# One add fewer on VectorE, two accumulating matmuls more on TensorE, in three deferred layer norms of a decoder step

## What is computed

```python
def _layernorm(x, g, b):
    xf = x.astype(F32)
    mu = jnp.mean(xf, axis=-1, keepdims=True)
    var = jnp.mean(jnp.square(xf - mu), axis=-1, keepdims=True)
    return ((xf - mu) * lax.rsqrt(var + EPS) * g + b).astype(x.dtype)

for layer in range(DEPTH):
    m, ... = _mixer_ab(x, ...) if layer % 2 == 0 else _mixer_cd(x, ...)
    x = _layernorm(DN_ALPHA * x + m, ln_g[layer, 0], ln_b[layer, 0])
    x = _layernorm(DN_ALPHA * x + _ffn(x, ...), ln_g[layer, 1], ln_b[layer, 1])
```

## Time and profile before

| | before |
|---|---|
| median of 3 runs | 1396.12 us (1396.09 to 1396.78) |
| profiled execution | 1397.7 us, its span 1395.9 us |
| mean granted TensorE clock | 0.989 |
| TensorE busy | 1342.1 us (96%) |
| VectorE busy | 815.0 us (58%) |
| ScalarE busy | 452.0 us (32%) |
| GpSimd busy | 594.2 us (43%) |

### The profile page before, as it was taken

One profiled execution on the slowest core, in us unless ns is written; L12 is line 12 of the kernel. 1 busy time (PEld: TensorE's weight loads), 2 busy tenths in 40 slices (PEclk: granted clock), 3 DMA queues, 4 the chain that ended last, 5 costly groups with the idle time before them and its releaser, 6 DMA issues.

```text
span 1395.9 us, 28685 instructions
## 1 busy us (share of the span) xinstructions
PE 1342.1 (96%) x11696; PEld 1268.9 (91%) x11696; DVE 815.0 (58%) x1007; ACT 452.0 (32%) x600; POOL 594.2 (43%) x256
## 2 busy tenths in 40 slices
PE   7999999999999999999899989989999999999994
PEld 7999999999999999999799964469999999999994
DVE  3256775797655553223758999837787555540045
ACT  3332233433333332213423234434443333331132
POOL 2342333355555554343323344004365555554351
PEclk9999999999999999999999999999999999999998
DMA  6222231323333232222788989942222222232301
GB/s 245 61 87 67 77 92 50 94 65 107 79 107 92 90 118 86 101 71 76 275 284 265 329 277 342 360 196 82 86 76 90 90 90 90 90 125 83 99 26 62
DMA packets 84429, 180.81 MB, mean 130 GB/s; under 512 B 25977, under 2 KB 25978, under 8 KB 83842
## 3 DMA queue, kind: packets, MB, share of 16 engines
q1 hardware_dynamic: 83666, 175.82, 38.5%
q0 software_dynamic: 688, 3.92, 0.9%
HBM read 173.66 MB, written 6.05 MB: 129 GB/s over the span
## 4 chain that ended last, share of the span: by engine, by line
PE 86%; DVE 10%; ACT 2%; issue 1%; DMA 1%; SPq 0%; ACTq 0%; DVEq 0%
PE ps L1064 75%; DVE pj L2284 3%; PE ps L1443 2%; PE ps L1211 1%; PE ps L1560 1%; DVE sq L1777 1%; DVE sq L1775 1%; PE ps L1414 1%; PE ps L1545 1%; DMA raw<-in_w_ab_in 1%; ACT sq L541 0%; PE ps L1534 0%; DVE tiny L2358 0%; PE ps L1315 0%; ACT wh L436 0%
## 5 line engine op out<-in xcount | busy, mean ns | idle before, releaser
L900 POOL TENSOR_TENSOR wl<-raw,wh 128x1024 fp32r<-128x1024 f32 (+1 forms) x179 | 492.3, 2750 | 623.7 <-ACT wh L436 623.7
L1064 PE MATMUL ps<-xh,wh 128*128 128x260 f32 x2112 | 436.1, 288 | 16.0 <-DVE xl L1826 9.7
L1064 PE MATMUL ps<-xl,wh 128*128 128x260 f32 x2112 | 430.0, 285 | 0.0
L1064 PE MATMUL ps<-xh,wl 128*128 128x260 f32 x2112 | 429.5, 285 | 0.0
L436 ACT ACTIVATE wh<-raw 128x1024 fp32r<-128x1024 f32 (+1 forms) x179 | 200.0, 1117 | 558.3 <-PE ps L1064 557.5
L1064 PEld LDWEIGHTS ps<-xh,wh 128*128 128x128 f32 x2112 | 331.2, 191 | 22.6 <-issue 16.4
L1064 PEld LDWEIGHTS ps<-xl,wh 128*128 128x128 f32 x2112 | 331.0, 190 | 0.0
L1064 PEld LDWEIGHTS ps<-xh,wl 128*128 128x128 f32 x2112 | 329.7, 190 | 0.0
L1064 PE MATMUL ps<-hh,wh 128*128 128x260 f32 x704 | 142.1, 283 | 0.0
L1064 PE MATMUL ps<-hh,wl 128*128 128x260 f32 x704 | 141.6, 282 | 0.0
L1064 PE MATMUL ps<-hl,wh 128*128 128x260 f32 x704 | 141.3, 282 | 0.0
(11 more groups left out here) (348 smaller groups left out, 1508.7 us busy)
## 6 DMA issues: line engine op xcount, KB each, us to landing
raw<-in_w_f_in SPq DMA_DIRECT2D x88, 512.0 KB, 3.6
pages<-in_cache_kt SPq DMA_DIRECT2D x128, 256.0 KB, 4.2
pages<-in_cache_v SPq DMA_DIRECT2D x128, 256.0 KB, 4.2
raw<-in_w_f_out SPq DMA_DIRECT2D x32, 704.0 KB, 4.0
raw<-in_w_ab_in SPq DMA_DIRECT2D x23, 512.0 KB, 3.6
raw<-in_w_cd_in SPq DMA_DIRECT2D x20, 512.0 KB, 5.1
raw<-in_w_ab_out SPq DMA_DIRECT2D x8, 512.0 KB, 3.5
raw<-in_w_cd_out SPq DMA_DIRECT2D x8, 512.0 KB, 6.2
```

What stands on the lines that cost most here:

```text
L900: nc.gpsimd.tensor_tensor(wl[:, j % SPLIT, 0:b * P], raw[:, j, 0:b * P], wh[:, j % SPLIT, 0:b * P].bitcast(F32), ALU.subtract).then_inc(w_ ...
L1064: mm = nc.tensor.matmul(out[h], w[:, slot, block_at * P:block_at * P + P], rows[k][:, HT * h:end if h else HT], start=start and a, stop=st ...
```

## The change

VectorE stops one add earlier: it signals ln_sq_added once two rows are left (the add of L1776). TensorE multiplies ones with both rows, one after the other in the same accumulator, so `square_sums` has four matmuls in place of two. This happens in the norms before f0_in, cd_in and f1_in. Nothing else is different, and no other instruction changes place.

```diff
                 pe.wait_ge(ln_sq_added, LN_OF[idx] + 1)
                 for h in range(2):
-                    mm = nc.tensor.matmul(ps[:, 4 + h, 0:HT], ones, sq[:, 0, HT * h:HT * h + HT], start=True, stop=True)
+                    for k in range(2):
+                        mm = nc.tensor.matmul(ps[:, 4 + h, 0:HT], ones, sq[:, k, HT * h:HT * h + HT], start=k == 0, stop=k == 1)
                 mm.then_inc(ln_var, 1)
...
                 link(V.tensor_tensor(sq[:, 0:4, :], sq[:, 0:4, :], sq[:, 4:8, :], ALU.add))
-                link(V.tensor_tensor(sq[:, 0:2, :], sq[:, 0:2, :], sq[:, 2:4, :], ALU.add))
-                V.tensor_tensor(sq[:, 0, :], sq[:, 0, :], sq[:, 1, :], ALU.add).then_inc(ln_sq_added, 1)
+                V.tensor_tensor(sq[:, 0:2, :], sq[:, 0:2, :], sq[:, 2:4, :], ALU.add).then_inc(ln_sq_added, 1)
```

## The result

The changed kernel takes 1392.59 us (median of 22 runs, 1390.02 to 1397.92), the kernel before 1396.91 us (22 runs, 1395.09 to 1401.77): ratio 0.9968 with a 95% interval of 0.9959 to 0.9977, so 3.2 to 5.7 us faster, 4.5 in the middle. Runs of one kernel differ by several microseconds, more than the three runs at hand for the prediction had shown. The profiled execution took 1392.94 us, its span is 4.8 us shorter than that of before.

A forecast was written before the change was run, and what follows sets the result against it. TensorE, busy 1342.1 us, bounds the kernel, so only its waits or added work count. Gains of 0.69 + 1.33 + 0.69 = 2.7 us take the median from 1396.12 to 1393.4 us, range 1391.6 to 1395.2.

The forecast's parts named there:

- The place: At the sums of squares in f0_in, cd_in and f1_in: 2.44 us before, 1.745 after, TensorE 0.69 us further on each.
- The waits at tile 6 stay: In f0_in and f1_in VectorE's chain moves 0.69 us with TensorE, so the 1.28 us waits at tile 6 remain.
- cd_in (1.33 us): L1443 starts 1.33 us earlier: 0.69 from the sums, 0.64 from VectorE's chain, with L2173 held by GpSimd's next L900.
- The clock: At L1443 in cd_in: falls to 1.2 GHz behind a 2.75 us wait as before, 1.46 us still lost.
- Clock kept: Rival, chance 0.15: cd_in's shorter wait leaves TensorE at 2.4 GHz, 4.2 us gained, 1391.9.
- The scatter: Spread of the runs shown for the whole kernel, 0.7 us, used in the forecast's own range 1392.7 to 1394.1.
- how the chances were divided at 0.2%: Whole kernel: 2.8 us is distinguishable from no change; faster 0.46, same 0.47, slower 0.07.
- Second add held: Rival, chance 0.03: L1776 starts after GpSimd's L900 and is held, 1.4 us lost per norm, 4.3 in all, 1400.4.
- Not what it says: Rival, chance 0.04: L1178's wait is for a bank or ScalarE and stays, 2.6 us added, 1398.7.
- Eaten by the second wait: Rival, chance 0.16: VectorE's chain meets another hold, TensorE waits longer at L1443 and tile 6; 1394.0 to 1395.4.

The follow-up runs named there:

- the run in which GpSimd waits: Kernel before, three adds and two matmuls kept, but GpSimd's subtraction for the second round's first slot waits for ln_sq_added: 1393.54 us against 1397.88, ratio 0.9973.
- the kernel with four rows: Changed kernel with only VectorE's first add kept and eight matmuls summing four rows: 1397.44 us against 1397.88 for the kernel before, ratio 0.9998.

## Why the prediction was right, and where it was off

**The number.** 1392.59 us is close to the 1393.4 forecast, but luck has a part in that: the kernel before took 1396.91 us beside it and not 1396.12, and the gain is 4.5 us (3.2 to 5.7) where 2.7 was forecast. What was right is the mechanism, place by place.

**The place (0.69 us each): right.** 0.71 us in f0_in and 0.68 in f1_in, each up to tile 6, and 0.69 in cd_in, up to TensorE's arrival at the key slots. The removed add was held by GpSimd, shown by the run in which GpSimd waits (0.70 us). The matmuls cost 0.435 us each, shown by 1.745 us for four and, in the kernel with four rows, 0.44 for each one more.

**The waits at tile 6 stay: right.** 1.26 us each against 1.28 in f0_in and 1.27 in f1_in; 2.5 us for both in the waits, as before.

**cd_in (1.33 us): right, 1.39.** The small adds came when the hold ended and L2173 was caught by the next L900, as forecast. I had the adds held; it was the copy ahead of them, L2191, with one input. The time is the same.

**The clock: the step that was off.** I let the clock fall behind 2.75 us because that is nearer to 3.39 than to 1.3. It fell in 5 of 8 such standstills, and in the profiled execution it didn't. "Clock kept", which I had at 0.15, is neither the rule nor an exception, and an average over runs contains it in part. 2.82 + 0.55 = 3.4 us, inside the interval of 3.2 to 5.7, near its low end. What the middle, 4.5, holds beyond that isn't explained by any run; executions differ by up to 4 us in the attention stretch alone and by 3 us before the first norm (start to the add in f0_in 270.7 to 274.1 us in these traces), and the four sets of runs of the kernel before have medians 1.4 us apart, so it may well be chance. That is argued, not shown.

**The scatter** was taken from three runs (0.7 us). Over 22 runs it is some 7 us. The forecast itself doesn't hang on it, but how the chances were divided at 0.2% does: with gains of clock and scatter on either side, that line was drawn too finely.

**The rivals.** Second add held: no. It starts 1.20 us ahead of L900, as before. Not what it says: the wait is gone with the add. Eaten by the second wait: not in the changed kernel, but the GpSimd run and the one with four rows show the mechanism in cd_in, the first with a copy held and the second with GpSimd 0.05 us ahead.

## What to carry to other kernels

When an instruction on VectorE takes several times what its size wants, look for a GpSimd operation that began before it and ended just ahead of its end, by about the work that its size wants (0.55 us for 520 columns). Taking the instruction out, or letting GpSimd wait for it, is worth the hold and not the work. In f0_in and f1_in letting GpSimd wait gave 1.6 us a place and taking the add out 0.7, since the latter pays with 0.87 us of TensorE's time. In cd_in it was the other way round, 0.7 against 1.4, because the later subtraction held something else. So a hold moved can be a hold kept: trace what the freed engine meets next. And before forecasting a fraction of a per cent, measure how far runs of the same kernel lie apart.

## What was not expected of the hardware

- A copy of 64 columns with a single SBUF input (L2191) was held by GpSimd's subtraction like the adds with two: 1.48 us instead of 0.13.
- Ties are decided by hundredths of a microsecond and can cost 2.2 us (three scalings in 4.13 instead of 1.92, GpSimd 0.05 us ahead). In f0_in of the kernel before, GpSimd's third L900 began at 291.92 and VectorE's scaling at 291.97 was held for it (2.92 us). In the changed kernel they began at 290.59 and 290.62, the scaling took 0.69 us and that L900 2.98 instead of 2.40: VectorE seems to have been let through. It had no consequence at tile 6.
- The same standstill of 2.69 us is followed by 1.2 GHz in some executions and by 2.4 in others of the same kernel, worth 1.3 to 1.6 us up to the second key slots.
